# Allocating the shared SBUF tiles of a two-part transformer kernel in another order

## The reference, cut to what matters

```
for l in range(2):          # first half
    h = rms_norm(x) * (1 + sc1) + sh1
    x = x + g1 * hybrid_mixer(h)      # h @ w_in, retention and HGRN2, @ w_out
    h = rms_norm(x) * (1 + sc2) + sh2
    x = x + g2 * ((silu(conv(h @ w_gate)) * (h @ w_val)) @ w_down)
x = rms_norm(x, final_norm_w)
for i in range(2):          # second half
    h = rmsnorm(x)                    # h @ w_in: window attention and RWKV7
    x = x + rmsnorm(mixed @ w_out)
    h = rmsnorm(x)
    x = x + rmsnorm((gelu(ua) * ub) @ w_down)    # ua, ub = conv(h @ w_up)
    x = x + rmsnorm(sigmoid(x @ w_ple_gate) * (p @ w_ple))
```

## Time and profile before

| | before |
|---|---|
| median of 3 runs | 4173.47 us (4164.61 to 4181.4) |
| profiled execution, its own time | 4173.47 us |
| its span, first to last instruction | 4171.7 us |
| instructions | 70239 |
| TensorE (PE) busy | 3868.6 us, 93% of the span |
| VectorE (DVE) busy | 2112.0 us, 51% |
| ScalarE (ACT) busy | 1712.1 us, 41% |
| GpSimd (POOL) busy | 794.6 us, 19% |
| granted TensorE clock, mean | 0.982 |

### The profile page before, as it was taken

The page is one execution under the profiler, slowest core; times in us unless marked ns, Lnnn a source line. Parts: engine busy times, 40 slices in busy tenths (PEclk is TensorE's granted clock), DMA queues, the critical chain, the costliest instruction groups (busy, mean ns, idle before and its releaser), DMA issues.

```text
span 4171.7 us, 70239 instructions
## 1 busy us (share of the span) xinstructions
PE 3868.6 (93%) x29148; PEld 3135.1 (75%) x29148; DVE 2112.0 (51%) x3719; ACT 1712.1 (41%) x2512; POOL 794.6 (19%) x1108
## 2 busy tenths in 40 slices
PE   5898999999899999999999999998999999989997
PEld 4676778777678877877787778876777787778885
DVE  5575662126533227366664376325546666356603
ACT  3264422336443236445443332235644444342223
POOL 1111222221122221210001222221120000222221
PEclk9999999999999999999999999999999999999998
DMA  8855998975489985832223879986572222679995
GB/s 282 236 118 106 272 292 188 199 171 120 95 175 193 191 172 119 177 86 66 53 52 87 182 161 195 193 183 146 115 170 66 52 55 57 142 153 196 193 191 130
DMA packets 189741, 628.75 MB, mean 151 GB/s; under 512 B 22768, under 2 KB 27888, under 8 KB 189040
## 3 DMA queue, kind: packets, MB, share of 16 engines
q0 software_dynamic: 158976, 549.52, 61.0%
q1 hardware_dynamic: 27888, 70.53, 4.9%
q10 hardware_dynamic: 2560, 4.20, 0.3%
HBM read 612.63 MB, written 2.10 MB: 147 GB/s over the span
## 4 chain that ended last, share of the span: by engine, by line
PE 42%; DVE 10%; ACT 6%; DMA 2%; issue 2%; SPq 0%; DVEq 0%; ACTq 0%; POOL 0%
PE bank L228 11%; PE bank L230 10%; PE bank L229 10%; PE bank L1954 4%; ACT L2112 1%; ACT gate L2112 1%; PE bank L1642 1%; PE bank L1624 1%; DVE rw_z L2371 1%; PE bank L1943 1%; ACT w L2112 1%; PE bank L2015 1%; ACT acc L2112 1%; PE bank L1615 1%; DVE x L392 1%
## 5 line engine op out<-in xcount | busy, mean ns | idle before, releaser
L228 PE MATMUL bank<-h_hi,w_hi 128*128 128x512 f32 x2608 | 1065.7, 409 | 46.4 <-DMA w_lo<-in_b_wup 7.9
L230 PE MATMUL bank<-h_hi,w_lo 128*128 128x512 f32 x2608 | 1024.6, 393 | 0.0
L229 PE MATMUL bank<-h_lo,w_hi 128*128 128x512 f32 x2608 | 1024.4, 393 | 0.0
L161 ACT ACTIVATE w_lo<-w_hi 128x1024 fp32r<-128x1024 f32 (+2 forms) x552 | 556.0, 1011 | 1002.5 <-DMA w_hi<-in_a_wgv 301.8
L228 PEld LDWEIGHTS bank<-h_hi,w_hi 128*128 128x128 f32 x2608 | 494.5, 190 | 180.5 <-issue 57.2
L229 PEld LDWEIGHTS bank<-h_lo,w_hi 128*128 128x128 f32 x2608 | 495.1, 190 | 106.5 <-issue 10.5
L230 PEld LDWEIGHTS bank<-h_hi,w_lo 128*128 128x128 f32 x2608 | 494.4, 190 | 106.9
L2112 ACT ACTIVATE gate<-bank 128x512 f32<-128x512 f32 x80 | 47.8, 597 | 277.1 <-PE bank L1954 277.1
L228 PE MATMUL bank<-fa_y_hi,w_hi 128*128 128x512 f32 x352 | 137.1, 390 | 1.8 <-DMA w_lo<-in_a_wd 1.8
L228 PE MATMUL bank<-fb_y_hi,w_hi 128*128 128x512 f32 x352 | 137.0, 389 | 0.7 <-DMA w_lo<-in_b_wd 0.7
L229 PE MATMUL bank<-fb_y_lo,w_hi 128*128 128x512 f32 x352 | 136.9, 389 | 0.0
(11 more groups left out here) (461 smaller groups left out, 7661.7 us busy)
## 6 DMA issues: line engine op xcount, KB each, us to landing
w_hi<-in_a_wgv POOLq DMA_DIRECT2D x80, 512.0 KB, 5.3
w_lo<-in_a_wgv POOLq DMA_DIRECT2D x80, 512.0 KB, 7.6
w_hi<-in_b_wup POOLq DMA_DIRECT2D x80, 512.0 KB, 5.2
w_lo<-in_b_wup POOLq DMA_DIRECT2D x80, 512.0 KB, 7.4
w_hi<-in_a_wh POOLq DMA_DIRECT2D x48, 512.0 KB, 4.7
w_lo<-in_a_wh POOLq DMA_DIRECT2D x48, 512.0 KB, 5.7
fa_ada_raw<-in_ada SPq DMA_DIRECT2D x48, 512.0 KB, 7.9
w_hi<-in_b_wrkv POOLq DMA_DIRECT2D x48, 512.0 KB, 4.9
```

Source lines behind the costliest of these rows:

```text
L161: st.do(st.eng.activation(self.lo[:, s], self.hi[:, s].bitcast(F32), ACT.Copy, scale=-1.0), (self.neg_made, n + 1))
L228: pe.matmul(out, self.hi[:, a], hh[:, k0 + k, :], start=first and k == 0, stop=False)
L229: pe.matmul(out, self.hi[:, a], hl[:, k0 + k, :], start=False, stop=False)
L230: mm = pe.matmul(out, self.lo[:, a], hh[:, k0 + k, :], start=False, stop=last and k == ks - 1)
```

## The change

Only the order in which `Run.__init__` asks for its tiles changes. No tile changes its size or type, and no other function is touched.

```
--- before
+++ after
@@ Run.__init__
         self.x = sb("x", [P, KD, S])
-        self.c_act, self.mods = sb("c_act", [P, KD]), sb("mods", [P, DEPTH, 48])
-        self.scale, self.final_w = sb("scale", [P, KD]), sb("final_w", [P, KD])
+        self.c_act, self.scale, self.final_w = sb("c_act", [P, KD]), sb("scale", [P, KD]), sb("final_w", [P, KD])
+        self.hh, self.hl = sb("h_hi", [P, KD, S], F32R), sb("h_lo", [P, KD, S], F32R)
+        self.w, self.acc, self.rstd = sb("w", [P, 3, S]), sb("acc", [P, S]), sb("rstd", [P, S])
+        self.mods = sb("mods", [P, DEPTH, 48])
         self.ones, self.eye = sb("ones", [P, P]), sb("eye", [P, P])
         self.eps, self.spare = sb("eps", [P, 4]), sb("spare", [P, 4])
         self.par_a, self.par_b = sb("par_a", [P, DEPTH, A_N]), sb("par_b", [P, DEPTH, B_N])
-        self.b_sin = sb("b_sin", [P, S])
-        self.hh, self.hl = sb("h_hi", [P, KD, S], F32R), sb("h_lo", [P, KD, S], F32R)
-        self.w, self.acc, self.rstd = sb("w", [P, 3, S]), sb("acc", [P, S]), sb("rstd", [P, S])
-        self.b_cos = sb("b_cos", [P, S])
+        self.b_cos, self.b_sin = sb("b_cos", [P, S]), sb("b_sin", [P, S])
```

## The result

| | before | changed |
|---|---|---|
| median | 4173.47 us | 4200.05 us |
| lowest to highest of 7 runs each | 4164.61 to 4181.4 | 4191.27 to 4203.62 |
| ratio to before, 95% interval | 1 | 1.0061 (1.0051 to 1.0072) |
| profiled execution: time, span | 4173.47, 4171.7 us | 4194.59, 4192.8 us |

The changed kernel is slower by 0.61%, 26.6 us, a fraction of a per cent that nonetheless stands clear of the noise. It lies 1 us outside the range of the prediction, 4148 to 4199 us, on the side of the rival that had 0.08.

A forecast was written before the change was run, and what follows sets the result against it. The prediction took the rate of the large TensorE matmuls as the bound: 4173.5 + 0 (VectorE, ScalarE) + 0 (DMA) + 0 (TensorE) = 4173.5 us. Likeliest time 4173 us, range 4148 to 4199, no change 0.80.

The forecast's parts named there:

- the rival that had 0.08: Large TensorE matmuls: the new places make weight and activation reads collide, 4227 us at 6.2 ns per matmul; chance 0.08.
- The failed step: TensorE's large matmuls: the new relative places of activations and weights cost 0, within bounds of -114 and +53 us.
- The slower rival: Large TensorE matmuls: new places collide, steps on `h_hi` alone reach 0.229 us or more, 4227 us; chance 0.08.
- price of 6.2 ns: Extra step time behind short TensorE matmuls, 232.9 against 226.7 ns; over 8592 matmuls it gives 53 us.
- threshold of 2.4 ns: Loss per TensorE step from which 8592 matmuls make the kernel slower by 0.5%, 21 us.
- The plain float32 pair: TensorE product of `ones` at 96 and `w` at 352: matmuls 0.43 us apart, hardly a nanosecond for unequal places.
- The 13.3 ns: Part of each 226.7 ns TensorE step beyond 512 columns at 2.4 GHz; 114 us over 8592 matmuls if it went away.
- The faster rival: Large TensorE matmuls: equal places were a collision, step falls to 213.3 ns, 4060 to 4100 us expected; chance 0.10.
- VectorE and ScalarE, 0: Instructions on moved tiles keep their durations: 0 taken, 3 us either way kept for the range.
- DMA, 0: Seven prologue transfers write moved tiles, no stream has a moved source or target: 0 taken, bound 1 us.
- Ring and stages at the same bytes: Ring and stage tiles do not shift, the last shared tile ends at 85344 either way; a shift was given nothing.
- Clock: TensorE's half-clock stretches might move, 1.6 us each, 13 needed for 0.5%; chance 0.02 with the like, half each way.

The follow-up runs named there:

- run 9: Small matmul-only kernel: activations' start pushed by fine distances, other column counts and types tried; fp32r 238.0 ns a step at 4 bytes, bf16 215.8 ns.
- run 5: Small kernel with only the three `Weights.blocks` matmuls, activations pushed 0 to 480 bytes from the weights: 226.7 ns a step at 0 and 256, 233.4 at 128.
- run 6: Against the kernel before, `h_hi`, `h_lo`, `w`, `acc`, `rstd` put at 96 within 512 bytes, 256 from the ring: 4175.48 us, ratio 1.0008.
- run 10: Small matmul-only kernel, `h_hi`, `h_lo` and `w_lo` each pushed 0 to 224 bytes against `w_hi`, 512 mixes: none below 226.67 ns, one at 226.68.
- run 2: Against the kernel before, only `h_hi` and `h_lo` moved, to 224 within 512 bytes as in the changed kernel: 4196.64 us, ratio 1.0064.
- run 4: Against the kernel before, `h_hi`, `h_lo` and the ring all at 224 within 512 bytes, stage tiles left at 352: 4197.9 us, ratio 1.006.
- run 8: Against the kernel before, the ring moved to 224 within 512 bytes (also `w`, `acc`, `rstd`), `h_hi`, `h_lo` and stage tiles at 352: 4218.73 us, ratio 1.0111.
- run 3: Against the kernel before, only `w`, `acc` and `rstd` moved to 224 within 512 bytes, `h_hi` and `h_lo` at 352: 4170.31 us, ratio 0.9998.
- run 1: Against the kernel before, `h_hi`, `h_lo`, `w`, `acc`, `rstd` in the changed kernel's low place, but at 352 within 512 bytes: 4170.72 us, ratio 0.9997.

## Why the prediction was wrong

- **The failed step** is the one on TensorE: "I take 0 between -114 and +53, because the step is the same to about a nanosecond over the distances of tiles that the trace has, which is what a cost per matmul would give and not what a collision would." The constancy of the steady steps was true and worth nothing. As the same paragraphs say, every fp32r product before stands at the same remainder of 512, so the trace never varied what the change varies. Measured in its place: moving `h_hi` and `h_lo` to 128 bytes from the ring costs 4.9 ns on each of some 7970 full-clock steps, 39 us of TensorE, 26.6 us of time.
- **The slower rival** had the right sign, and the step it named as its mark, 0.229 us or more on `h_hi` alone. That the cause is a collision of two reads is argued, see below. Its price of 6.2 ns was near the 4.9 measured, but by luck as far as the runs show: it comes from the stretch behind short matmuls, where both operands stand at equal places, and no run shows that this slower stretch (5.3 ns from the unrounded starts) is the same effect. Its threshold of 2.4 ns was passed, and its +53 us held as a bound; it was too high as a forecast by counting all 8592 matmuls as full-clock and all as on the path. What was wrong was its chance of 0.08, and a range that ended 1 us short.
- **The plain float32 pair** The earlier trace rows was called a weak witness, and was none: run 9 shows that form blind to the distance, and its two places, 96 and 352, are 256 bytes apart, which runs 5 and 6 show to cost nothing for fp32r either. The table of places goes by 512 bytes, where the period is 256.
- **The 13.3 ns** were not to be won. Nothing is below the 226.67 ns of equal places, in the distances of runs 5 and 9 and in the 512 mixes of run 10. What the 13.3 ns are stays open. The faster rival's argument that they vanish at half clock is true (426.4 ns), but says nothing on whether a placement wins them.
- **The Trainium skill's two rules.** The Trainium skill says that a step is N / 2.4 GHz plus 2.5 ns (TensorE: Matmul & The Clock Gate, section "Wait - 56ns, not 53.3ns?"). Run 9 agrees in bf16, 215.8 ns, but no fp32r group of 512 columns does at any distance. The Trainium skill also says that TensorE's two read ports are independent and that it never waits for anyone (SBUF - State Buffer, section "Who interferes with whom"). That would have kept the sum; runs 2, 4 and 8, where the place of one operand against the other sets the step, speak against it for fp32r.
- **VectorE and ScalarE, 0**: right, medians the same, run 3 the same time. **DMA, 0**: right, run 1 moves the same constants and costs nothing. **Ring and stages at the same bytes**: right, but this is just what made `h` lose its partner.
- **Clock**: 0.982 and 0.98 in the two profiled executions; the mean is 0.980 over 24 executions of the changed kernel and 0.980 over 23 of the kernel before. It has no part in the difference.

What stays open: why a relative start modulo 256 bytes slows fp32r alone, of the three types tried. Two reads that fall into the same part of the memory would fit, since a step of fp32r takes four bytes per column in 226.7 ns where float32 takes 429.2 ns for one matmul, and since at half clock the loss is gone; that is argued, no run shows the memory's inside. It would still have to explain three results: nothing is lost at 256 columns (run 9), `h_lo` alone costs more than `h_hi` alone (run 5), and one unequal mix costs nothing (run 10).

## What to carry to other kernels

For fp32r matmuls of 512 columns that are the bound, start the activations' and the weights' tiles at the same byte modulo 256; a small tile in between can cost 2 to 3% of each such step (4.9 of 227.6 ns in this kernel, 6.7 of 226.7 in run 5). Before a placement is called free, ask whether the trace holds a single pair of tiles with the new relation: a spread of zero over pairs that are all alike is no evidence. And a loss per matmul reaches the end in full only in stages where TensorE has no gaps, here about two thirds of it in all.

## What the runs showed of the hardware that I had not expected

- fp32r, 128 x 128 weights, 512 columns, full clock: 226.67 ns per matmul at distance 0 or 256, 228.9 at 64, 231.6 at 16, 231.0 at 80, 233.2 to 234.2 at most others, 238.0 at 4 bytes (runs 5 and 9). At half clock 426.4 to 426.5 ns both before and after.
- What counts is the start of the activations against that of the weights: it acted the same for `h_hi` at 32992 and for `fb_y_hi` behind 118112 (232.4 and 233.1 ns, the changed kernel and run 4), and also when TensorE is the only engine at work (run 5). The loss of a mix is not a sum of prices per matmul.
- bf16 (215.8 ns) and plain float32 (429.2 ns for each of its two matmuls) did not depend on it at 0, 64 and 128, nor does fp32r lose by it at 256 columns (120.0 ns at 0, 117.8 at 64, 118.6 at 128).
- With 32 weight columns a step is longer, not shorter, 231.6 ns at distance 0.
